# Delta rule's scan: the next batch's inverse ahead of the last merge, and the keys' turns next to the whole products

## The chip, the cores and the metric

One Trainium2 chip, one of its cores. The time is what one execution of the whole program takes on the device, in microseconds; the median of three runs is compared.

## What is computed

A trunk of two mixing layers over 1024 latent and 256 context tokens of width 1024, all in float32. The first layer has two branches, the second branch being a delta rule (RWKV-7) with 8 heads of 64, run once forward and once backward. Cut to what matters here:

```python
def rwkv_scan(inputs, S):
    def step(S, xs):
        r, v, kk, w, k, a = xs
        sa = jnp.einsum('bhvk,bhk->bhv', S, -kk)
        S = S * w[:, :, None, :] + sa[..., None] * (kk * a)[:, :, None, :] + v[..., None] * k[:, :, None, :]
        return S, jnp.einsum('bhvk,bhk->bhv', S, r)

    S, ys = lax.scan(step, S, tuple(jnp.moveaxis(t, 2, 0) for t in inputs))
    return jnp.moveaxis(ys, 0, 2), S
```

Each token rewrites a 64 x 64 state per head; the result is the state read by r. Everything else of the two layers (projections, the other scans, a long convolution, norms, output products) is in the program too and is not touched.

## The kernel before

The program is a row of stages, each with one block of code per engine; TensorE, VectorE, ScalarE and GpSimd take their instructions in the order in which that engine's block writes them, and wait on semaphores. `stage_rwkv_scan` runs twice, for d = 0 (forward) and d = 1 (backward). It takes the 1280 tokens in chunks of 64, two chunks (lanes 0 and 1) make a batch b, and there are 10 batches to a direction. 8 heads lie as 4 pairs j times 2 halves q of the partitions, so most products are groups of 8 or 16 matmuls of 64 x 64; in the trace a float32 matmul of this kind counts twice.

Inside a chunk the delta rule is a triangular system. Its inverse is built level by level for both lanes of a batch at once. Two buffers hold `inv` (upper and lower form), by b % 2. For batch b:

- `products(b, lane)` (TensorE, lines 1572 and 1578): keys times queries into the banks TURN and TURN + 1, and the strictly triangular products into STRICT. VectorE's `read_products` (line 1791) masks the first into `prod`.
- `begin_inverse(b, lane)` (VectorE, lines 1798, 1803 twice, 1806): copies the strict products out and sets level 0 of the inverse. It needs the products of its own batch and lane and `inv` filled by GpSimd.
- five levels n: `half_product(b, n)` (TensorE, line 1649), `copy_half` (ScalarE, line 1717), `whole_products(b, n)` (TensorE, line 1661, and for n < 5 line 1667), then `merge_upper` and `merge_lower` (VectorE, lines 1810 and 1814, predicated copies).
- `turns(b, lane)` (TensorE): four transposes of the keys into TURN (line 1590) and four of v into TURN + 1 (line 1594); ScalarE copies them out in `copy_keys` (line 1721) and `copy_v` (line 1726).

While batch b's inverse is built, the state is carried through batch b - 1, one lane in each half of the batch: `begin_chunk` (the states' products, line 1611), VectorE's `add_rest` (line 1822), `solve_chunk` (line 1620), ScalarE's `copy_u` (line 1738), `end_chunk` (lines 1629, 1634, 1638), VectorE's `update_state` (lines 1827, 1828). `pull(b)` (line 1602, copied by line 1733) prepares the next batch's right side. For d = 1 VectorE also adds the outputs (`add_y`, line 1835), for d = 0 ScalarE copies them (line 1744).

The order of the work is written out by hand in the loops over b at the end of each engine's block. The two waits that the change touches are these:

```python
pe.wait_ge(products_read, 4 * (b + 1) if lane == 0 else min(4 * (b + 1) + 2, 2 * N))   # ahead of the keys' turns
pe.wait_ge(level0_ready, 2 * (b + 1))                                                  # before half_product(b, 1)
```

`products_read` counts two for every `read_products`: lane 0's keys' turns wait for the reads of batch b, lane 1's for those of batch b + 1, lane 0, whose matmuls wrote the same bank. `level0_ready` counts one for every `begin_inverse`, so the first half product of a batch waits for both lanes' starts.

Of the kernel before, what the change touches and what calls it, by code (L numbers as in the profile page):

```python
# [19 lines left out]
P = 128  # L20
# [1452 lines left out]
def stage_rwkv_scan(p, arena, d, operands, v_dram, vT, chunk_decay, y):  # L1473
# [6 lines left out]
    nc = p.nc  # L1480
    C, J = R_CHUNK, R_PAIRS
# [3 lines left out]
    N = len(steps)  # L1485
    B = N // 2
# [7 lines left out]
    products_read = p.semaphore("r_products_read")  # L1494
# [8 lines left out]
    keys_turned = p.semaphore("r_keys_turned")  # L1503
# [18 lines left out]
    with ExitStack() as local:  # L1522
# [23 lines left out]
        with nc.Block() as block:  # L1546
# [13 lines left out]
            def _(pe):  # L1560
# [18 lines left out]
                                                keys(s)[part(q), j, q, :], start=True, stop=True)  # L1579
                    last.then_inc(strict_ready, 1)  # L1580

                def turns(b, lane):
                    s, c = 2 * b + lane, steps[2 * b + lane]

                    if d == 0 and s == 0:
                        pe.wait_ge(v_loaded, 32)
                        pe.wait_ge(pads_cleared, 2)
                    pe.wait_ge(products_read, 4 * (b + 1) if lane == 0 else min(4 * (b + 1) + 2, 2 * N))
                    for j in range(J):
                        last = nc.tensor.transpose(bank(TURN)[:, j * P:(j + 1) * P],  # L1590
                                                   keys(s)[:, j].rearrange("p k t -> p (k t)"), p.const("ident"))
                    last.then_inc(keys_turned, 1)
                    for j in range(J):
                        last = nc.tensor.transpose(bank(TURN + 1)[:, j * P:(j + 1) * P], vT[:, j, c * C:c * C + 2 * C], p.const("ident"))
                    last.then_inc(v_turned, 1)
# [77 lines left out]
                for b in range(B):  # L1673
                    half_product(b, 1)
                    if b:
                        begin_chunk(b - 1, 0)
                    whole_products(b, 1)
                    if b:
                        solve_chunk(b - 1, 0)
                    turns(b, 0)  # L1680
                    half_product(b, 2)
                    if b:
                        end_chunk(b - 1, 0)
                    whole_products(b, 2)
                    if b + 1 < B:
                        products(b + 1, 0)
                    half_product(b, 3)
                    if b:
                        begin_chunk(b - 1, 1)
                    whole_products(b, 3)  # L1690
                    if b:
                        solve_chunk(b - 1, 1)
                    turns(b, 1)
                    half_product(b, 4)
                    if b:
                        end_chunk(b - 1, 1)
                    whole_products(b, 4)
                    if b + 1 < B:
                        products(b + 1, 1)
                    half_product(b, 5)  # L1700
                    pull(b)
                    whole_products(b, 5)
# [73 lines left out]
            @block.vector  # L1776
            def _(dve):
                made = [0]

                def then(instruction):  # L1780
                    made[0] += 1
                    instruction.then_inc(chain, 1)
                    dve.wait_ge(chain, made[0])

                def read_products(b, lane):
                    s = 2 * b + lane
                    dve.wait_ge(products_ready, s + 1)
                    if b >= 2:
                        dve.wait_ge(outputs_ready, s - 3)
                    for q in range(2):  # L1790
                        nc.vector.tensor_tensor(prod[:, b % 2, lane, q], paired(bank(TURN + q)), product_mask(q), ALU.mult).then_inc(products_read, 1)

                def begin_inverse(b, lane):
                    s = 2 * b + lane
                    dve.wait_ge(strict_ready, s + 1)
                    if b >= 2:
                        dve.wait_ge(half_ready, TOP * (b - 1))
                    nc.vector.tensor_tensor(strict_t[:, b % 2, lane], narrow(bank(STRICT)[:, lane * HALF:(lane + 1) * HALF]),
                                            strict, ALU.mult).then_inc(strict_read, 1)
                    dve.wait_ge(inverse_filled, b + 1)  # L1800
                    dve.wait_ge(products_read, 2 * (s + 1))
                    for q in range(2):
                        nc.vector.copy_predicated(inv[part(q), b % 2, 0, lane], added(0, 0, J)[part(q)],
                                                  prod[part(q), b % 2, lane, q, :, part(q)])
                    dve.wait_ge(strict_read, s + 1)
                    nc.vector.copy_predicated(inv[:, b % 2, 1, lane], added(0, 1, J), strict_t[:, b % 2, lane]).then_inc(level0_ready, 1)  # L1806

                def merge_upper(b, n):
                    dve.wait_ge(upper_ready, TOP * b + n)
                    nc.vector.copy_predicated(flat(inv[:, b % 2, 0]), added(n, 0, 2 * J), narrow(bank(UPPER))).then_inc(upper_merged, 1)  # L1810

                def merge_lower(b, n):
                    dve.wait_ge(lower_ready, (TOP - 1) * b + n)
                    nc.vector.copy_predicated(flat(inv[:, b % 2, 1]), added(n, 1, 2 * J), narrow(bank(LOWER))).then_inc(lower_merged, 1)

                def add_rest(b, lane):
                    s = 2 * b + lane
                    dve.wait_ge(rest_ready, s + 1)
                    dve.wait_ge(pulled_copied, b + 1)
                    if s:  # L1820
                        dve.wait_ge(u_summed, s)
                    nc.vector.tensor_tensor(rest[:, :, :], pulled[:, lane], narrow(bank(CHAIN)[:, 0:HALF]), ALU.add).then_inc(rest_copied, 1)

                def update_state(b, lane):
                    s, c = 2 * b + lane, steps[2 * b + lane]
                    dve.wait_ge(update_ready, s + 1)
                    then(nc.vector.tensor_tensor(state[:, :, :], state[:, :, :], narrow(bank(CHAIN)[:, 0:HALF]), ALU.add))
                    nc.vector.tensor_tensor(
                        state[:, :, :], state[:, :, :], chunk_decay[:, :, c].unsqueeze(2).broadcast_to([P, J, C]), ALU.mult).then_inc(state_ready, 1)

                def add_y(b, lane):
                    if d == 1:
                        c = steps[2 * b + lane]
                        dve.wait_ge(outputs_ready, 2 * b + lane + 1)
                        nc.vector.tensor_tensor(y[:, c], y[:, c], narrow(bank(OUT)[:, 0:HALF]), ALU.add).then_inc(y_copied, 1)

                nc.vector.memset(state[:, :, :], 0.0).then_inc(state_ready, 1)
                dve.wait_ge(masks_loaded, 16)
                for lane in range(2):
                    read_products(0, lane)  # L1840
                    begin_inverse(0, lane)
                for b in range(B):
                    if b:
                        add_rest(b - 1, 0)
                    merge_upper(b, 1)
                    merge_lower(b, 1)
                    if b:
                        update_state(b - 1, 0)
                    merge_upper(b, 2)
                    merge_lower(b, 2)  # L1850
                    if b:
                        add_y(b - 1, 0)
                    if b + 1 < B:
                        read_products(b + 1, 0)
                    if b:
                        add_rest(b - 1, 1)
                    merge_upper(b, 3)
                    merge_lower(b, 3)
                    if b:
                        update_state(b - 1, 1)  # L1860
                    if b + 1 < B:
                        begin_inverse(b + 1, 0)
                    merge_upper(b, 4)
                    merge_lower(b, 4)
                    if b:
                        add_y(b - 1, 1)
                    if b + 1 < B:
                        read_products(b + 1, 1)
                    merge_upper(b, 5)
                    if b + 1 < B:  # L1870
                        begin_inverse(b + 1, 1)
                for lane in range(2):
                    add_rest(B - 1, lane)
                    update_state(B - 1, lane)
                    add_y(B - 1, lane)
# [1223 lines left out]
```

## Time and profile before

| | us |
|---|---|
| median of 3 runs | 3166.31 (3166.16 to 3173.97) |
| the profiled execution | 3175.72 |
| its span in the trace | 3173.9 |
| TensorE busy | 2769.6 (87% of the span) |
| VectorE busy | 1346.6 (42%) |
| ScalarE busy | 797.9 (25%) |
| GpSimd busy | 126.3 (4%) |

The profile is that of one execution. Its page gives for each engine the busy time, then groups of instructions by line with the time that the engine was idle just before them and what ended that idle time. The timeline gives single instructions in order; where many of one kind follow one another it merges them, with their number. PE is TensorE's matmuls, PEld its weight loads, DVE VectorE, ACT ScalarE, POOL GpSimd, and SPq the queue that issues transfers. The two directions of the scan lie between about 1010 and 1620 us of the span; the first full batches run from 1023 on (d = 0) and from 1327 on (d = 1).

### The profile page before, as it was taken

To read this page: it belongs to the slowest core of one execution; us is meant where nothing else is said; L and a number is where in the kernel's file an instruction comes from. 1 tells how busy PE (TensorE), PEld (TensorE's weight loads), DVE (VectorE), ACT (ScalarE), POOL (GpSimd) and SP (SyncE) were. 2 spreads that over 40 slices of the span, in tenths; PEclk is the share of its full clock that TensorE was granted. 3 is DMA by queue.
4 is the path that set the end of the run, shared out by engine and by line. 5 is a ranking of instruction groups with operands and counts; after the bars stand their busy time and mean duration, and the time that the engine had idled before them with its cause. 6 is when DMAs were issued, how large, how long until landed. Compare 5 with 4: busy or idle time off the path is not lost. (4 is left out here: it accounts for less than half of the span.)

```text
span 3173.9 us, 52024 instructions
## 1 busy us (share of the span) xinstructions
PE 2769.6 (87%) x23220; PEld 1767.4 (56%) x23220; DVE 1346.6 (42%) x2127; ACT 797.9 (25%) x1422; POOL 126.3 (4%) x133
## 2 busy tenths in 40 slices
PE   7899999998996898788847987996877999989678
PEld 2454566665453888788844423442433768677643
DVE  3220444433774554455560232224342566656614
ACT  2111222253563222222221021011100333343311
POOL 0000000000222000000001000002100000000000
PEclk9899999998997999899978997996988999999879
DMA  6200211112567110111014361101103000010033
GB/s 231 75 27 5 63 45 45 53 47 86 137 166 177 49 43 17 63 36 37 16 68 179 106 239 66 53 0 32 53 27 98 27 21 21 1 40 1 14 146 93
DMA packets 89788, 214.65 MB, mean 68 GB/s; under 512 B 6245, under 2 KB 45285, under 8 KB 85978
## 3 DMA queue, kind: packets, MB, share of 16 engines
q1 hardware_dynamic: 79854, 173.97, 15.9%
q0 software_dynamic: 9712, 37.36, 4.6%
q8 instruction: 183, 3.00, 0.4%
q14 instruction: 39, 0.32, 0.0%
HBM read 156.26 MB, written 55.05 MB: 67 GB/s over the span
## 5 line engine op out<-in xcount | busy, mean ns | idle before, releaser
L689 PE MATMUL psum<-arena,m_fill_weight 128*128 128x512 f32 (+1 forms) x864 | 335.5, 529 | 5.9 <-DMA m_fill_weight<-in_l_w_in 5.9
L2307 PE MATMUL psum<-arena,g_weight 128*128 128x512 f32 (+1 forms) x512 | 222.7, 562 | 26.1 <-DMA g_weight<-in_l_w_in 26.1
L389 PE MATMUL psum<-arena,project_weight_y 128*128 128x512 f32 x512 | 221.4, 595 | 13.0 <-DMA project_weight_y<-in_l_w_in 13.0
L689 PEld LDWEIGHTS psum<-arena,m_fill_weight 128*128 128x128 f32 x864 | 157.1, 193 | 108.2 <-issue 91.8
L389 PEld LDWEIGHTS psum<-arena,project_weight_y 128*128 128x128 f32 x512 | 97.8, 191 | 137.4 <-issue 122.8
L389 PE MATMUL psum<-arena,project_weight_m 128*128 128x512 f32 (+3 forms) x432 | 156.6, 525 | 14.9 <-DMA project_weight_m<-in_l_w_in 14.9
L2553 DVE COPY_PREDICATED g_pairs<-g_masks,psum 128x512 f32<-128x512 uint8 x128 | 93.5, 730 | 147.6 <-PE psum L2335 147.6
L1649 PE MATMUL psum<-r_inv,r_strict_t 64*64 64x64 f32 x3200 | 114.9, 222 | 46.8 <-DVE r_inv L1806 46.8
L1166 PE MATMUL psum<-gp_weight,arena 128*128 128x512 f32 x320 | 149.9, 617 | 0.0
L2298 PE MATMUL psum<-g_weight,arena 128*128 128x128 f32 x1152 | 145.0, 275 | 0.0
L2057 PE MATMUL psum<-out_weight,arena 128*128 128x512 f32 x256 | 115.0, 613 | 28.1 <-DMA out_weight<-in_l_w_out 28.1
L2066 PE MATMUL psum<-out_weight,arena 128*128 128x512 f32 x320 | 137.7, 592 | 0.0
L1717 ACT COPY r_half<-psum 128x512 f32<-128x512 f32 x100 | 58.5, 585 | 313.8 <-PE psum L1649 313.8
L2298 PEld LDWEIGHTS psum<-g_weight,arena 128*128 128x128 f32 x1152 | 136.7, 192 | 0.0
L1649 PEld LDWEIGHTS psum<-r_inv,r_strict_t 64*64 64x64 f32 x3200 | 102.9, 136 | 56.5 <-DVE r_inv L1806 49.7
L2307 PEld LDWEIGHTS psum<-arena,g_weight 128*128 128x128 f32 x512 | 92.2, 200 | 74.1 <-issue 49.8
L389 PEld LDWEIGHTS psum<-arena,project_weight_m 128*128 128x128 f32 (+1 forms) x432 | 82.0, 190 | 90.1 <-issue 69.1
L1661 PE MATMUL psum<-r_half,r_inv 64*64 64x64 f32 x3200 | 121.4, 229 | 12.2 <-ACT r_half L1717 12.0
L2335 PEld LDWEIGHTS psum<-arena 128*128 128x128 f32 x896 | 120.3, 205 | 16.9 <-issue 15.7
L2335 PE MATMUL psum<-arena 128*128 128x128 f32 x896 | 127.2, 289 | 0.0
L2099 DVE TENSOR_TENSOR out_res<-psum,out_gate 128x1024 f32<-128x1024 f32 x18 | 22.0, 1224 | 233.7 <-PE psum L2057 147.5
L1810 DVE COPY_PREDICATED r_inv<-r_masks,psum 128x512 f32<-128x512 uint32 x100 | 72.8, 728 | 113.5 <-PE psum L1661 113.5
(382 smaller groups left out, 4338.2 us busy)
## 6 DMA issues: line engine op xcount, KB each, us to landing
mod_weight<-in_l_mod_w SPq DMA_DIRECT2D x16, 1536.0 KB, 7.7
arena<-scratch_operands SPq DMA_DIRECT2D x40, 512.0 KB, 3.6
scratch_operands<-arena POOLq DMA_DIRECT2D x16, 640.0 KB, 8.2
scratch_operands<-arena POOLq DMA_DIRECT2D x32, 320.0 KB, 11.2
g_weight<-in_l_w_in SPq DMA_DIRECT2D x20, 512.0 KB, 4.3
m_fill_weight<-in_l_w_in SPq DMA_DIRECT2D x18, 512.0 KB, 3.8
out_weight<-in_l_w_out SPq DMA_DIRECT2D x16, 512.0 KB, 11.4
project_weight_y<-in_l_w_in SPq DMA_DIRECT2D x4, 2048.0 KB, 7.9
```

Of the source, the lines that this page charges most:

```text
L389: last = nc.tensor.matmul(p.psum[0:rows, u % 8, 0:n], lhsT, rhs, start=(k == 0), stop=(k == KT - 1))
L689: last = nc.tensor.matmul(p.psum[:, FILL + f % BANKS, 0:width], weight[:, q % PIECES, k, :], hT[:, k, at:at + width], start=(k == 0), stop ...
L1166: last = nc.tensor.matmul(p.psum[:, PROJECT + u % 2, :], hT[:, k, t * P:(t + 1) * P], weight[:, job, k, :], start=(k == 0), stop=(k == KT ...
L1649: last = nc.tensor.matmul(bank(H_BANK)[part(q), at(lane, j)], strict_t[part(q), b % 2, lane, j, :], inv[part(q), b % 2, 0, lane, j, :], st ...
L1661: last = nc.tensor.matmul(bank(UPPER)[part(q), at(lane, j)], inv[part(q), b % 2, 1, lane, j, :], half[part(q), lane, j, :], start=True, st ...
L1810: nc.vector.copy_predicated(flat(inv[:, b % 2, 0]), added(n, 0, 2 * J), narrow(bank(UPPER))).then_inc(upper_merged, 1)
L2057: last = nc.tensor.matmul(p.psum[:, 2 * i + n, :], lhsT, weight[:, k, n * BANK:(n + 1) * BANK], start=(k == 0), stop=(k == KT - 1))
L2066: last = nc.tensor.matmul(p.psum[:, 2 * (i % 4) + n, :], lhsT, weight[:, k, n * BANK:(n + 1) * BANK], start=(k == 0), stop=(k == KT - 1))
L2298: last = nc.tensor.matmul(bank[:, (t - part[0]) * P:(t - part[0] + 1) * P], hT[:, kk, t * P:(t + 1) * P], w[:, kk, :], start=(kk == 0), st ...
L2307: last = nc.tensor.matmul(bank[:, 0:width], w[:, kk, :], hT[:, kk, first:first + width], start=(kk == 0), stop=(kk == KT - 1))
L2335: last = nc.tensor.matmul(p.psum[:, SCORES + m % RING, (c - 4 * g) * C:(c - 4 * g + 1) * C], left, right, start=True, stop=True)
L2553: nc.vector.copy_predicated(pairs[:, w % 2, 4 * g:4 * g + 4, :], mask(units[w][1], n), chunked(p.psum[:, SCORES + m % RING, :])).then_inc( ...
```

## The change

Two edits, both of order. No instruction is new and none is gone.

- `turns` is cut in two: `turn_keys` (with its wait for `products_read`) and `turn_v` (with the waits for v's load and the cleared pads, for the first chunk of d = 0). In each half of a batch `turn_keys` now stands ahead of `whole_products(b, 1)` and `whole_products(b, 3)`, and `turn_v` stays behind `solve_chunk`, where both stood.
- On VectorE `begin_inverse(b + 1, 1)` stands ahead of `merge_upper(b, 5)`, no longer behind it.

```diff
-                def turns(b, lane):
-                    s, c = 2 * b + lane, steps[2 * b + lane]
-
-                    if d == 0 and s == 0:
-                        pe.wait_ge(v_loaded, 32)
-                        pe.wait_ge(pads_cleared, 2)
+                def turn_keys(b, lane):
+                    s = 2 * b + lane
                     pe.wait_ge(products_read, 4 * (b + 1) if lane == 0 else min(4 * (b + 1) + 2, 2 * N))
                     for j in range(J):
                         last = nc.tensor.transpose(bank(TURN)[:, j * P:(j + 1) * P],
                                                    keys(s)[:, j].rearrange("p k t -> p (k t)"), p.const("ident"))
                     last.then_inc(keys_turned, 1)
+
+                def turn_v(b, lane):
+                    s, c = 2 * b + lane, steps[2 * b + lane]
+
+                    if d == 0 and s == 0:
+                        pe.wait_ge(v_loaded, 32)
+                        pe.wait_ge(pads_cleared, 2)
                     for j in range(J):
@@ TensorE's loop, lane 0; the same for lane 1 around whole_products(b, 3)
                     if b:
                         begin_chunk(b - 1, 0)
+                    turn_keys(b, 0)
                     whole_products(b, 1)
                     if b:
                         solve_chunk(b - 1, 0)
-                    turns(b, 0)
+                    turn_v(b, 0)
                     half_product(b, 2)
@@ VectorE's loop
                     if b + 1 < B:
                         read_products(b + 1, 1)
+                        begin_inverse(b + 1, 1)
                     merge_upper(b, 5)
-                    if b + 1 < B:
-                        begin_inverse(b + 1, 1)
```

VectorE's queue at the end of a batch, before (r_prod is the masked product, r_strict_t the strict products, r_inv the inverse, r_rest the right side for the solve):

```order
L1791 TENSOR_TENSOR r_prod<-psum,r_masks 128x512 x2
L1810 COPY_PREDICATED r_inv<-r_masks,psum 128x512
L1798 TENSOR_TENSOR r_strict_t<-psum,r_masks 128x256
L1803 COPY_PREDICATED r_inv<-r_masks,r_prod 64x256 x2
L1806 COPY_PREDICATED r_inv<-r_masks,r_strict_t 128x256
L1822 TENSOR_TENSOR r_rest<-r_pulled,psum 128x256
```

The same place in the changed kernel, whose VectorE lines lie 5 further down (1791 is 1796):

```order
L1796 TENSOR_TENSOR r_prod<-psum,r_masks 128x512 x2
L1803 TENSOR_TENSOR r_strict_t<-psum,r_masks 128x256
L1808 COPY_PREDICATED r_inv<-r_masks,r_prod 64x256 x2
L1811 COPY_PREDICATED r_inv<-r_masks,r_strict_t 128x256
L1815 COPY_PREDICATED r_inv<-r_masks,psum 128x512
L1827 TENSOR_TENSOR r_rest<-r_pulled,psum 128x256
```

The merge of level 5 (1810, now 1815) went from ahead of begin_inverse's four instructions to behind them.

TensorE's queue from the first half product of a batch to the second, before (consts is the identity of a transpose, arena holds the keys, r_vT v):

```order
L1649 MATMUL psum<-r_inv,r_strict_t 64x64 x16
L1611 MATMUL psum<-r_state,arena 64x64 x8
L1661 MATMUL psum<-r_half,r_inv 64x64 x16
L1667 MATMUL psum<-r_inv,r_half 64x64 x16
L1620 MATMUL psum<-r_rest,r_inv 64x64 x8
L1590 MATMUL psum<-consts,arena 128x128 x4
L1594 MATMUL psum<-consts,r_vT 128x128 x4
L1649 MATMUL psum<-r_inv,r_strict_t 64x64 x16
```

The same place in the changed kernel (1649 is 1652 now, 1590 is 1586):

```order
L1652 MATMUL psum<-r_inv,r_strict_t 64x64 x16
L1614 MATMUL psum<-r_state,arena 64x64 x8
L1586 MATMUL psum<-consts,arena 128x128 x4
L1664 MATMUL psum<-r_half,r_inv 64x64 x16
L1670 MATMUL psum<-r_inv,r_half 64x64 x16
L1623 MATMUL psum<-r_rest,r_inv 64x64 x8
L1597 MATMUL psum<-consts,r_vT 128x128 x4
L1652 MATMUL psum<-r_inv,r_strict_t 64x64 x16
```

The four transposes of the keys went from behind the solve to between the states' products and the whole products; those of v stayed. ScalarE's, GpSimd's and the transfers' queues have the same order in both kernels.

## Rows read from the trace of the kernel before

**Rows 1.** The page's costliest groups: line, tiles, shape, count | busy, mean ns | idle before.
```profile
L1649 PE MATMUL psum<-r_inv,r_strict_t 64*64 64x64 f32 x3200 | 114.9, 222 | 46.8 <-DVE r_inv L1806 46.8
...
L1661 PE MATMUL psum<-r_half,r_inv 64*64 64x64 f32 x3200 | 121.4, 229 | 12.2 <-ACT r_half L1717 12.0
```

**Rows 2.** Timeline, TensorE: start, length, operation, count [idle before <- releaser].
```profile
1051.96 1.15 PE L1649 MATMUL psum<-r_inv,r_strict_t 64*64 64x64 f32 x32 [2.39 <-DVE r_inv L1806]
...
1080.05 1.15 PE L1649 MATMUL psum<-r_inv,r_strict_t 64*64 64x64 f32 x32 [2.39 <-DVE r_inv L1806]
...
1081.88 1.97 PE L1661 MATMUL psum<-r_half,r_inv 64*64 64x64 f32 x32
...
1109.36 1.15 PE L1649 MATMUL psum<-r_inv,r_strict_t 64*64 64x64 f32 x32 [2.39 <-DVE r_inv L1806]
...
1583.91 1.15 PE L1649 MATMUL psum<-r_inv,r_strict_t 64*64 64x64 f32 x32 [2.39 <-DVE r_inv L1806]
```

**Rows 3.** Windows, two batches: PE, PEld, DVE, ACT, POOL busy; PEclk; DMA share; GB/s.
```profile
1052.00:1080.00 28.00, 25.22 (x720) 23.63 (x720) 14.45 (x27) 8.37 (x18) 1.05 (x1) 1.00 0.13 41
1080.00:1109.30 29.30, 26.70 (x720) 25.13 (x720) 14.44 (x27) 8.37 (x18) 1.05 (x1) 0.94 0.12 39
```

**Rows 4.** Timeline, all engines, a batch's end in the second direction.
```profile
1407.65 1.27 DVE L1791 TENSOR_TENSOR r_prod<-psum,r_masks 128x512 f32<-128x512 f32 x2
...
1409.48 1.15 PE L1661 MATMUL psum<-r_half,r_inv 64*64 64x64 f32 x32
...
1409.60 0.58 ACT L1733 COPY r_pulled<-psum 128x512 f32<-128x512 f32 x1 [0.18 <-PE psum L1602]
...
1410.67 0.72 DVE L1810 COPY_PREDICATED r_inv<-r_masks,psum 128x512 f32<-128x512 uint32 x1 [1.75 <-PE psum L1661]
...
1411.29 0.41 DVE L1798 TENSOR_TENSOR r_strict_t<-psum,r_masks 128x256 f32<-128x256 f32 x1
...
1412.51 0.45 DVE L1806 COPY_PREDICATED r_inv<-r_masks,r_strict_t 128x256 f32<-128x256 uint32 x1
...
1413.01 1.15 PE L1649 MATMUL psum<-r_inv,r_strict_t 64*64 64x64 f32 x32 [2.39 <-DVE r_inv L1806]
```

**Rows 5.** Timeline, VectorE, the last merge of a batch, first direction.
```profile
1077.71 0.72 DVE L1810 COPY_PREDICATED r_inv<-r_masks,psum 128x512 f32<-128x512 uint32 x1 [2.08 <-PE psum L1661]
```

**Rows 6.** Timeline, all engines, the second lane's piece of that batch.
```profile
1394.73 1.16 PE L1572 MATMUL psum<-arena 64*128 64x128 f32 x16
...
1395.94 1.29 DVE L1791 TENSOR_TENSOR r_prod<-psum,r_masks 128x512 f32<-128x512 f32 x2
...
1397.27 0.63 PE L1611 MATMUL psum<-r_state,arena 64*64 64x64 f32 x16
...
1397.48 0.58 ACT L1717 COPY r_half<-psum 128x512 f32<-128x512 f32 x1 [4.67 <-PE psum L1649]
...
1398.12 1.15 PE L1661 MATMUL psum<-r_half,r_inv 64*64 64x64 f32 x32 [0.22 <-ACT r_half L1717]
...
1399.10 1.10 PE L1667 MATMUL psum<-r_inv,r_half 64*64 64x64 f32 x32
...
1400.04 0.63 PE L1620 MATMUL psum<-r_rest,r_inv 64*64 64x64 f32 x16
...
1400.60 0.66 PE L1590 MATMUL psum<-consts,arena 128*128 128x128 f32 x4
...
1401.09 0.60 PE L1594 MATMUL psum<-consts,r_vT 128*128 128x128 f32 x4
...
1401.49 0.58 ACT L1721 COPY r_k_tok<-psum 128x512 f32<-128x512 f32 x1
...
1401.62 0.97 PE L1649 MATMUL psum<-r_inv,r_strict_t 64*64 64x64 f32 x26
...
1402.82 0.59 ACT L1717 COPY r_half<-psum 128x512 f32<-128x512 f32 x1 [0.74 <-PE psum L1649]
```

**Rows 7.** Timeline, TensorE, first batch of the second direction.
```profile
1341.65 1.15 PE L1661 MATMUL psum<-r_half,r_inv 64*64 64x64 f32 x32 [0.69 <-ACT r_half L1717]
```

More of the change, by code:

```diff
@@ L1689, in _ @@
                         begin_chunk(b - 1, 1)
+                    turn_keys(b, 1)
                     whole_products(b, 3)
@@ L1692, in _ @@
                         solve_chunk(b - 1, 1)
-                    turns(b, 1)
+                    turn_v(b, 1)
                     half_product(b, 4)
```

## The prediction

> **What bounds the kernel now.** I read the page first, for the share of the engines. TensorE is busy for 87% of the span (table above), so anything that shortens TensorE's queue, or a stall of it, counts in full unless another engine is close behind. I then went to the groups of instructions [rows 1]. Two groups of the scan's matmuls have idle time of TensorE before them: 46.8 us before the half products of line 1649, released by VectorE's line 1806 (the last step of begin_inverse), and 12.2 us before the whole products of line 1661, released by ScalarE's copy of line 1717. Those two are what the edit aims at.
>
> The timeline of TensorE's queue says where the first one stands [rows 2]. From the second batch of a direction on, the first half product of each batch waits 2.39 us; there are 9 such waits in each direction, 18 in all, 43.0 us (the others are the two starts, 1.92 us each, that the change leaves). The starts of these rows also give the batch period: 28.09 us (1051.96 to 1080.05) for 12 batches and 29.2 to 29.4 for 6 (the first of them is 1080.05 to 1109.36, 29.31); of the 18 waits the row at 1051.96 is the first and that at 1583.91 the last. The six long ones differ in one thing [rows 3]: the granted clock is 0.94 over the batch, where it is 1.00 in its neighbour. In it the whole products that began at 1081.88, just after the wait of 2.39 us, took 1.97 us [rows 2] for what takes 1.15 in other batches [rows 6]: TensorE was at 1.2 GHz for a stretch, then at 2.4 again. I find such a fall in the six batches only, behind the same stall each time.
>
> The timeline of a batch's end shows why VectorE is late [rows 4]. It finishes the products' reads (line 1791, 1407.65 + 1.27 = 1408.92), then waits 1.75 us for the last whole products, merges them (line 1810), and only then takes begin_inverse, lines 1798 to 1806, from 1411.29 to 1412.96. TensorE starts the next batch at 1413.01. Nothing that begin_inverse reads comes from the last merge: its inputs were there when VectorE went idle. In the first direction, without add_y on VectorE, the idle stretch is longer, 2.08 us [rows 5].
>
> **The change part by part.** No instruction is added or removed on any engine; two pieces are moved, and no DMA is.
>
> *begin_inverse ahead of the last merge.* It takes 1412.96 - 1411.29 = 1.67 us [rows 4]. Put behind the reads it begins at about 1408.84 (on VectorE a follower starts some 0.08 us before the end of the row ahead, as line 1798 does behind 1810) and ends at 1410.51. The last whole products begin at 1409.48; a run of 32 such matmuls hands over after 0.98 us (1398.12 to 1399.10 [rows 6]), so TensorE is free at 1410.46. VectorE's signal, 0.05 us behind its end as now, comes at 1410.56. The half product then starts at 1410.56 where it started at 1413.01: 2.45 us in the second direction. In the first VectorE has 0.33 us more room, TensorE sets the start, and it gains 1413.01 - 1410.46 = 2.55. Sum: 9 x 2.45 + 9 x 2.55 = 45.0 us. The merge itself is pushed back by nothing: the whole products end at 1410.63 and VectorE is free at 1410.51, a cover of 0.12 us; were that cover gone, its result is first wanted by the next whole products (for the PSUM bank), about 2 us later (half products 0.98, states' products 0.56, keys' turns 0.49, as worked out below), while the merge takes 0.72. Behind the moved wait for the strict products stands only that merge; line 1578 has ended before the reads are over, so the wait is met.
>
> *The clock.* With the stall gone TensorE has at most 0.1 us of idle time there, and the six falls lose what preceded them. Each costs 29.31 - 28.09 = 1.22 us [rows 2]: 6 x 1.2 = 7.2 us. Bounds: 0 if the falls come anyway, 7.2 if none does. I take 7.2, since all six stand behind that stall and none elsewhere in a full batch.
>
> *The keys' turns.* One piece of a batch now [rows 6]: the states' products begin at 1397.27, whole products at 1398.12 (0.85 later; 0.22 of that waits for ScalarE's copy, 1397.48 + 0.58 = 1398.06), the second whole products 1399.10, the solve 1400.04, keys' turns 1400.60, v's turns 1401.09, the next half product 1401.62: 4.35 us. With the keys' turns moved: states' products 0.56 (a group of 16 as the solve: 1400.04 to 1400.60), keys' turns 0.49, whole 0.98 and 0.94, solve 0.56, v's turns 0.53: 4.06 us. The gain is 0.29 us, since 0.49 us of turns fill a hole of 0.29 and push the whole products back by 0.20. It happens twice in each of 18 batches: 36 x 0.29 = 10.4 us. Bounds: 0, if the later whole products are felt at once somewhere, and 36 x 0.49 = 17.6, if the turns were hidden whole. I take 10.4, which the starts give.
>
> Who might feel it? ScalarE: its copy of the keys (line 1721, behind that of u) ends at 1401.49 + 0.58 = 1402.07, and the next copy of a half product starts at 1402.82, after 0.74 us of idle time [rows 6]. The half product comes 0.49 us nearer to the solve, so 0.25 us of that room is left. The keys' turns now wait earlier for VectorE's reads of the other lane's products: these run from 1395.94 for 1.29 us, to 1397.23, and the turn is due at 1397.27 + 0.56 = 1397.83, 0.60 us of room. In the other lane the reads end at 1408.92 and the turn is due near 1412.1.
>
> *The first batch of a direction.* There is no states' product, and whole products wait 0.69 us [rows 7]; the turns fit into that hole. 4 turns x 0.49 = 2.0 us.
>
> **The sum**: 45.0 + 7.2 + 10.4 + 2.0 = 64.6 us. The profiled execution took 3175.7 us, which gives 3111.1. The median of the runs is 3166.31, 9.4 us less, and I take the difference as the same for both kernels: 3101.7. One of three runs of before was at 3173.97, so a median some 8 us higher is possible and belongs in the range.
>
> **A rule against it.** The keys' turns ran at the full clock: 4 of them took 0.66 us behind the solve and the half product behind them kept its pace [rows 6]. The Trainium skill (TensorE: Matmul & The Clock Gate, Part 4: PE-mode transpose) says that a transpose does not count as work for the clock gate as other matmuls do; the trace does not agree so far, and it is a rival below.
>
> **The rivals.**
> 1. *The keys' turns give nothing*, the rest works. ScalarE's 0.25 us of room is little. For it: four ScalarE operations follow one another there. Against: the room comes out positive with 0.25 us, and line 1717's copy takes 0.58 to 0.59 us each time [rows 6]. Time: 3101.7 + 12.4 = 3114. Chance 0.12.
> 2. *The stall is passed on.* TensorE starts earlier and meets another wait in the next piece, most likely the one for the pulled products or the rest. These are copied at 1409.60 + 0.58 = 1410.18 [rows 4], and wanted at 1410.56 + 0.98 = 1411.54, so 1.4 us of room speaks against it. If half of the 45 us came back, the time would be 3124, and with the falls of the clock too, 3131. Chance 0.07.
> 3. *The turns cost the clock.* If each keys' turn, now cut off from v's, brought one fall, 36 x 1.22 = 44 us would come back: 3146. Forty pairs of turns without a fall behind them speak against. Chance 0.03. It is the case that the page's rule would give.
> 4. *Slower: the keys' turn blocks TensorE's queue.* Its wait for VectorE's reads stands ahead of the whole products now, so a late read holds up all of the chain and with it the merges. Place: lane 1, room 0.60 us. To cancel 64.6 us over 18 batches it needs 3.6 us of stall each, so reads that end 4.2 us later than now; at 5 us later the time is 3101.7 + 18 x 4.4 = 3181. But the reads start 0.05 us behind the products' matmuls (1394.73 + 1.16 = 1395.89 [rows 6]), which stand on TensorE's own queue ahead of the turn, so a reader can hardly fall behind; I give it 0.01.
> 5. *The wait is not lifted*, since another semaphore holds the half product or begin_inverse. The order of both queues shows the move, the buffer of the fill by GpSimd and the strict products are done earlier; then only 12.4 us would be won, 3154. Chance 0.02.
>
> **How the numbers follow.** The forecast has 0.75; its own range is 3094 to 3110: 5 us for the keys' term, 7 for the clock, 8 for the spread of the runs. With rival 1 the range is 3093 to 3117, and what is left out is rivals 2 to 5, 0.13, and the tails. About 0.3% (9.5 us) is what a measurement of this kernel can tell from no change. Forecast and rivals 1, 2, 3 and 5 are all faster by more; rival 4 is slower; to no change I give 0.02 for gains eaten by something I don't see. Faster 0.97, same 0.02, slower 0.01.
>
> **What would show it.** In the profile after: no idle time of TensorE before the half products except at the two starts and at most 0.1 us in the second direction; VectorE idle ahead of the last merge near 0.1 us in the second direction and 0.4 in the first; no wait of the whole products on ScalarE's copy from the second batch on; batches of 25.0 us (28.09 - 2.5 - 0.6) in place of 28.09, all with a granted clock of 1.00. I am wrong if batches are longer than 25.5 us, if falls of the clock stay, or if a wait appears before the keys' turns.

## The result, and the profile after

The changed kernel took 3115.85 us (median of 4 runs, 3110.89 to 3121.62) beside 3170.14 us for the kernel before (4 runs, 3166.16 to 3175.87): ratio 0.9828, 95% interval 0.9801 to 0.9855. Three later comparisons of the same two kernels gave 3111.70 to 3173.23, 3114.34 to 3177.51 and 3109.91 to 3174.00, ratios 0.9804, 0.9806 and 0.9796. So the change is worth 54 to 64 us, against a forecast of 64.6. Direction and mechanism were right. The time of 3101.7 us was 8 to 14 us too low: 3115.85 lies outside the range of the forecast itself (3094 to 3110) and inside the wider one (3093 to 3117) that also takes in rival 1; the later medians, 3109.91 to 3114.34, lie on both sides of 3110.

The page of the changed kernel, costliest groups (line, tiles, shape, count | busy, mean ns | idle before), answers to [rows 1]; line 1649 is now 1652, line 1661 is 1664:

```profile
L1664 PE MATMUL psum<-r_half,r_inv 64*64 64x64 f32 x3200 | 115.6, 222 | 2.9 <-ACT r_half L1722 2.7
L1652 PE MATMUL psum<-r_inv,r_strict_t 64*64 64x64 f32 x3200 | 114.2, 222 | 3.8 <-DVE r_inv L1811 3.8
```

The idle time before the half products fell from 46.8 us to 3.8, which is the two starts (1.92 each) and nothing else; that before the whole products fell from 12.2 to 2.9, of which four waits of 0.69 us in the first batches are 2.7. The whole products' mean duration is lower too, 222 ns for 229 (the half products had 222 already): no stretch at half clock is left in the full batches. The windows over one batch of each direction show it (PE, PEld, DVE, ACT, POOL busy; PEclk; DMA share; GB/s), where [rows 3] had 25.2 to 26.7 us of work in 28.0 to 29.3:

```profile
1075.20:1100.40 25.20, 25.20 (x728) 23.55 (x724) 14.49 (x27) 8.37 (x18) 1.04 (x1) 1.00 0.13 45
...
1371.60:1397.00 25.40, 25.40 (x724) 23.66 (x722) 15.12 (x29) 7.62 (x16) 1.04 (x1) 1.00 0.14 45
```

TensorE is busy for all of it. The end of a batch, timeline of all engines, first direction (rows 1074.30 to 1075.49) and second (1370.48 to 1371.67), answers to [rows 4, 5]:

```profile
1074.30 1.15 PE L1664 MATMUL psum<-r_half,r_inv 64*64 64x64 f32 x32
...
1074.56 0.45 DVE L1811 COPY_PREDICATED r_inv<-r_masks,r_strict_t 128x256 f32<-128x256 uint32 x1
1075.28 1.10 PE L1652 MATMUL psum<-r_inv,r_strict_t 64*64 64x64 f32 x32
1075.49 0.73 DVE L1815 COPY_PREDICATED r_inv<-r_masks,psum 128x512 f32<-128x512 uint32 x1 [0.48 <-PE psum L1664]
...
1370.48 1.15 PE L1664 MATMUL psum<-r_half,r_inv 64*64 64x64 f32 x32
...
1371.07 0.45 DVE L1811 COPY_PREDICATED r_inv<-r_masks,r_strict_t 128x256 f32<-128x256 uint32 x1
1371.57 1.15 PE L1652 MATMUL psum<-r_inv,r_strict_t 64*64 64x64 f32 x32
1371.67 0.73 DVE L1815 COPY_PREDICATED r_inv<-r_masks,psum 128x512 f32<-128x512 uint32 x1 [0.15 <-PE psum L1664]
```

The last whole products hand over to the next batch's half products after 0.98 us in the first direction and 1.09 in the second, where VectorE's line 1811 ends at 1371.52, 0.05 us before the start. The merge is not later: it starts 1.19 us behind the start of the last whole products in both directions, as before (1409.48 to 1410.67), and VectorE has 0.48 and 0.15 us of idle time ahead of it.

The other piece, TensorE's timeline from one half product to the next, answers to [rows 6]:

```profile
1062.22 0.63 PE L1614 MATMUL psum<-r_state,arena 64*64 64x64 f32 x16
1062.79 0.66 PE L1586 MATMUL psum<-consts,arena 128*128 128x128 f32 x4
1063.37 1.15 PE L1664 MATMUL psum<-r_half,r_inv 64*64 64x64 f32 x32
1064.36 1.10 PE L1670 MATMUL psum<-r_inv,r_half 64*64 64x64 f32 x32
1065.29 0.63 PE L1623 MATMUL psum<-r_rest,r_inv 64*64 64x64 f32 x16
1065.85 0.65 PE L1597 MATMUL psum<-consts,r_vT 128*128 128x128 f32 x4
1066.44 0.97 PE L1652 MATMUL psum<-r_inv,r_strict_t 64*64 64x64 f32 x26
```

From the states' products to the next half product it is 4.22 us, where it was 4.35 and where the prediction had 4.06. The keys' turns, alone now, hand over after 0.58 us and v's after 0.59, not after 0.49 and 0.53 as they did side by side.

One more reading is needed before the experiments. I take the scan from the first to the last of ScalarE's 20 copies of the pulled products (line 1733, now 1738), one per batch. It lasted 556.9 us before (1048.55 to 1605.41) and 495.9 after (1049.21 to 1545.10): 61.0 us less. The profiled executions differ by 54.1 us (3175.72 and 3121.62), so about 7 us were lost outside that stretch. The stretch leaves out the first batch of the first direction, up to its copy, and takes in what lies between the two directions: 57.8 of the 61.0 us are in the nine intervals between copies of each direction, 3.2 between the two directions.

### The profile page after: what moved, and what is told of

It is laid out like the page before. It is cut to its first block and busy times, and to the rows that moved or that the text cites. A ratio compares the mean times of both kernels' runs of the same rounds, so it can differ in the third digit from the quotient of the medians.

```text
span 3119.8 us, 52024 instructions
## 1 busy us (share of the span) xinstructions
PE 2769.6 (89%) x23220; PEld 1760.4 (56%) x23220; DVE 1347.2 (43%) x2127; ACT 798.4 (26%) x1422; POOL 126.4 (4%) x133
## 5 line engine op out<-in xcount | busy, mean ns | idle before, releaser
L215 PE MATMUL psum<-mod_weight,mod_silu 128*2 128x512 f32 x192 | 90.2, 622 | 28.3 <-DMA mod_weight<-in_l_mod_w 28.3
```

The costliest lines, as they stand in the source:

```text
L215: last = nc.tensor.matmul(p.psum[0:2, g, :], silu[:, i, :], weight[:, i % SLOTS, g * BANK:(g + 1) * BANK], start=(i == 0), stop=(i == KT - 1))
```

## The experiments

The batch periods below are the intervals between those copies in each profile; a direction has 8 of them before its last, shorter one.

| kernel | median, us | before, measured beside it | ratio (95%) | periods, first direction | second direction | scan |
|---|---|---|---|---|---|---|
| before | | | | 28.09, three of 29.3 | 28.09, three of 29.2 to 29.5 | 556.9 |
| changed, again | 3111.70 | 3173.23 | 0.9804 (0.9789 to 0.9819) | 25.21 | 25.38 | 495.9 |
| inverse only | 3117.99 | 3173.23 | 0.9824 (0.9809 to 0.9839) | 25.48 | 25.65 | 502.6 |
| keys only | 3168.39 | 3173.23 | 0.9980 (0.9966 to 0.9994) | 27.81, five of 29.0 to 29.3 | 27.80, two of 29.3 | 553.6 |
| stall filled, 18 | 3200.23 | 3173.23 | 1.0082 (1.0067 to 1.0098) | 29.84 | 29.84 | 581.2 |
| stall filled, 10 | 3167.28 | 3174.00 | 0.9976 (0.9966 to 0.9986) | 28.10 | 28.10 | 547.4 |
| changed, third | 3114.34 | 3177.51 | 0.9806 (0.9786 to 0.9825) | 25.21 | 25.37 | 495.1 |
| pair in the hole | 3108.03 | 3177.51 | 0.9778 (0.9757 to 0.9798) | 24.62 | 24.79 | 484.7 |
| keys early | 3138.26 | 3177.51 | 0.9880 (0.9863 to 0.9897) | 26.49 | 26.66 | 519.3 |
| pair, sum late | 3107.08 | 3177.51 | 0.9782 (0.9764 to 0.9800) | 24.62 | 24.49 to 24.78 | 484.0 |
| changed, fourth | 3109.91 | 3174.00 | 0.9796 (0.9779 to 0.9813) | 25.21 | 25.38 | 496.1 |
| pair, again | 3110.34 | 3174.00 | 0.9793 (0.9775 to 0.9812) | 24.62 | 24.79 | 484.2 |

**The changed kernel again.** No edit.

> The changed kernel once more, on the same chip as the next three. Theory: the scan's batches repeat to 0.01 us (25.21 us in the first direction, 25.38 in the second, clock 1.00), so the scan is 61 us shorter than before again, and what the first profile lost outside the scan (7.0 us, of 54.1 us in all) is the spread of the other stages from execution to execution: it will be a different number here, between -5 and +8 us. Rival: the loss outside the scan belongs to the change (a shifted start of the later stages) and comes back as 6 to 8 us.

The scan was 495.9 us once more, with the same periods to 0.01 us. Span less scan was 2623.9 us in the first profile of this kernel (3119.8 - 495.9), and 2614.2, 2616.8 and 2611.3 in the three later ones: one kernel spreads over 12.6 us outside the scan. For the kernel before it was 2617.0, so the second profile of the change is 2.8 us below it. The 7 us lost in the first comparison belong to that spread; the rival, that the change itself causes them, is out.

**The inverse alone.** The diff to the kernel before:

```diff
                     if b + 1 < B:
                         read_products(b + 1, 1)
+                        begin_inverse(b + 1, 1)
                     merge_upper(b, 5)
-                    if b + 1 < B:
-                        begin_inverse(b + 1, 1)
```

> Before, with begin_inverse ahead of the last merge and the turns left together. Theory: the 18 waits of 2.39 us go (45 us) and the six falls of the clock with them (7 us): about 52 us under before, batches of 28.09 - 2.56 = 25.53 us in the first direction and 25.65 in the second, the waits of 0.22 us on ScalarE's copy still there. Rival: the two moves need each other, and a good part of the stall stays without the keys' turns: batches over 26 us.

55.2 us under before, with batches of 25.48 and 25.65 us. This one move is nearly all of the result. The waits on ScalarE's copy stayed, as the page's group of the whole products shows:

```profile
L1661 PE MATMUL psum<-r_half,r_inv 64*64 64x64 f32 x3200 | 116.5, 223 | 13.4 <-ACT r_half L1717 13.4
```

Their idle time is 13.4 us here, 12.2 before: it is longer because six of the waits had been swallowed by the falls of the clock. The rival, that the two moves need each other, is out.

**The keys' turns alone.** The changed kernel, with begin_inverse put back behind the last merge:

```diff
-                        begin_inverse(b + 1, 1)
                     merge_upper(b, 5)
+                    if b + 1 < B:
+                        begin_inverse(b + 1, 1)
```

> Before, with the keys' turns moved and begin_inverse left behind the last merge. Theory: the waits of 2.39 us stay, and falls of the clock behind them (four to eight in all); each half of a batch gains 0.13 to 0.20 us, not the predicted 0.29: batches of 27.76 us, 5 to 8 us under before with the first batches. Rival: the turns give the predicted 0.29 us twice when they are alone (batches of 27.51, 12 us under before), or nothing.

4.8 us under before; the batches without a fall of the clock are 27.81 us, 0.28 shorter. That is 0.14 us for each half of a batch, half of the predicted 0.29. The profile's list of waits has the 2.39 us untouched (us in total, times, longest):

```profile
PE psum L1652 <- DVE r_inv L1811: 46.8, 20, 2.4
```

Two of the 20 are the starts. With the stall still there the falls stay too: seven long periods among the 16, and the last one of the first direction also (26.14 where the second direction has 24.62), eight in all for the six of before. So the falls go with the stall, and not with the old place of the turns. Why 6 of 18 equal stalls bring a fall in one trace and 8 of 18 in the other, the runs do not show.

**The stall filled.** The kernel before, with matmuls whose result nobody uses in TensorE's queue at the place of the stall. Every output is computed as before.

```diff
                     if n == 1:
+                        if b:
+                            for i in range(18):
+                                nc.tensor.matmul(bank(H_BANK)[:, 0:P], p.const("ident"), p.const("ident"), start=True, stop=True)
                         pe.wait_ge(level0_ready, 2 * (b + 1))
```

> Before, with 18 matmuls of the identity (128 x 128, result not used) in TensorE's queue ahead of each batch's first half product, where it waits 2.39 us; the wait itself stays, since begin_inverse still ends when it does. Theory: the falls of the clock come from TensorE being without work there, so they vanish although the batch is no shorter than 28.09 us: all batches at 28.1 and clock 1.00, about 7 us under before. Rival: the falls have to do with the rhythm of the batches or of other work, and the six of 29.2 to 29.4 us stay, with a time as before.

This was a miss: 27.0 us slower where 7 us faster were expected. The trace counts 36 matmuls per batch at this line and they take 4.29 us, which is longer than the hole and makes every batch 29.84 us long, 1.75 us more than before:

```profile
1079.39 4.29 PE L1646 MATMUL psum<-consts 128*128 128x128 f32 x36
```

Of the falls it says the same already: no batch is longer than another by more than 0.01 us, and the clock is 1.00. The second attempt has `range(10)`.

> The filled stall with 10 matmuls in place of 18. The first filling took 4.2 us where the hole is 2.5 (each of these float32 matmuls shows as two of 0.12 us), so it made every batch 29.84 us. Ten take 2.4 us and fit. Theory: all batches at 28.1 us and clock 1.00, no falls, the scan 7 us shorter than before's. Rival: falls of the clock come back in some batches, as in the kernel before.

Timeline of all engines, end of a batch in the first direction:

```profile
1070.93 1.15 PE L1664 MATMUL psum<-r_half,r_inv 64*64 64x64 f32 x32
...
1072.01 2.50 PE L1646 MATMUL psum<-consts 128*128 128x128 f32 x20
...
1073.98 0.45 DVE L1809 COPY_PREDICATED r_inv<-r_masks,r_strict_t 128x256 f32<-128x256 uint32 x1
...
1074.49 1.15 PE L1652 MATMUL psum<-r_inv,r_strict_t 64*64 64x64 f32 x32
```

The half products still begin 0.06 us behind VectorE's line 1809, as in the kernel before, and 3.56 us behind the last whole products, where [rows 4] have 3.53. But TensorE has work in between. Windows over eight batches, the kernel before first, the filled one below it:

```profile
1048.50:1276.80 228.30, 206.35 (x5764) 193.90 (x5766) 115.62 (x216) 66.97 (x145) 8.37 (x8) 0.98 0.10 31
```

```profile
1043.00:1267.80 224.80, 221.31 (x5924) 207.83 (x5924) 115.75 (x216) 67.03 (x145) 8.37 (x8) 1.00 0.10 32
```

The clock is 1.00 over all of it, every period is 28.10 us, and the eight batches take 224.8 us for 228.3. Over the 18 periods of both directions this is 7.1 us, and the median is 6.7 us under before (interval of the ratio 0.9966 to 0.9986). The scan of this profile is 9.5 us shorter (547.4 for 556.9); the other 2.4 us lie between the directions, where no filling was added, and can't come from it. With 36 stalls filled in two traces and no fall, against 6 and 8 falls in 18 open stalls each, TensorE at 1.2 GHz was a consequence of its having nothing to do in the stall; work that is of no use is enough to keep it at 2.4 GHz. The Trainium skill (TensorE: Matmul & The Clock Gate, Part 1: The HAM clock gate) says that the default state is the throttled one and activity releases it; the fill runs agree (clock 1.00 over the eight batches with the filling, 0.98 without).

**The keys' turn one step earlier**, a dose of the rival that a wait blocks TensorE's queue. The diff to the changed kernel:

```diff
+                    turn_keys(b, 1)
                     half_product(b, 3)
                     if b:
                         begin_chunk(b - 1, 1)
-                    turn_keys(b, 1)
                     whole_products(b, 3)
```

> The changed kernel with lane 1's keys' turns one step earlier, ahead of the third half product. A dose of the rival that the keys' turn blocks TensorE's queue: VectorE's reads of the same bank end 0.94 us after the place. Theory: TensorE waits 0.94 us there in each batch, and the hole of 0.29 us ahead of the whole products opens again: 1.2 us per batch, 22 us over 18 batches; batches of 26.4 us. Rival: the wait is absorbed, since the levels of the inverse have slack elsewhere: under 5 us.

23.9 us slower than the changed kernel measured beside it, batches 1.28 us longer: about the theory's 22 and 1.2. The waits between 1060 and 1280 us name the place:

```profile
PE psum L1586 <- DVE r_prod L1796: 6.2, 8, 0.8
...
PEld psum L1664 <- ACT r_half L1722: 3.2, 9, 0.4
```

TensorE waits 0.8 us in each batch for VectorE's reads (0.94 was expected), nothing absorbs it, and the hole ahead of the whole products is open again. The mechanism of the slower rival is real, one step away from where the change put the turns; at the change's own place no such wait appears, so the room of 0.60 us holds.

**Both turns ahead of the whole products.** The diff to the changed kernel, the same in the other half of a batch:

```diff
                     turn_keys(b, 0)
+                    turn_v(b, 0)
                     whole_products(b, 1)
                     if b:
                         solve_chunk(b - 1, 0)
-                    turn_v(b, 0)
@@ turn_v
+                    if s:
+                        pe.wait_ge(v_copied, s)
```

The added wait keeps v's turns off a bank that ScalarE is still copying from, in the last batch.

> The changed kernel with v's turns moved too, right behind the keys' turns and ahead of the whole products. Theory: what the prediction missed is that a group of turns hands over to another group of turns after 0.49 us but to 64-row matmuls only after 0.58; with the turns adjacent again that is paid once per piece and not twice, so each piece takes 4.14 us where it takes 4.22: batches of 25.05 us, 3 us under the changed kernel. Rival: ScalarE has no room for a half product that comes a further 0.59 us nearer to the solve (its copy of the half product starts 0.3 us late), and the whole products of levels 2 and 4 wait: batches as now or longer.

Batches of 24.62 and 24.79 us, 0.59 us under the changed kernel where I expected 0.16 (25.05 us). TensorE's timeline of the piece:

```profile
1088.37 0.63 PE L1616 MATMUL psum<-r_state,arena 64*64 64x64 f32 x16
1088.93 0.66 PE L1586 MATMUL psum<-consts,arena 128*128 128x128 f32 x4
1089.43 0.60 PE L1599 MATMUL psum<-consts,r_vT 128*128 128x128 f32 x4
1089.96 1.15 PE L1666 MATMUL psum<-r_half,r_inv 64*64 64x64 f32 x32
1090.94 1.10 PE L1672 MATMUL psum<-r_inv,r_half 64*64 64x64 f32 x32
1091.87 0.63 PE L1625 MATMUL psum<-r_rest,r_inv 64*64 64x64 f32 x16
1092.34 0.93 PE L1654 MATMUL psum<-r_inv,r_strict_t 64*64 64x64 f32 x26
```

3.97 us, where the changed kernel has 4.22 and before 4.35; the rest of the 0.59 us lies behind it, from the half product to the next whole products, which takes 2.41 us (1092.34 to 1094.75) for 2.46 in each half of a batch. The turns side by side hand over after 0.50 and 0.53 again. What I had not counted is the other side: the solve hands over to a half product of its own shape after 0.47 us, and to turns after 0.56. So a switch between groups of 64 x 64 and of 128 x 128 costs some 0.05 to 0.1 us each way, and the change has four switches where the pair has two. It is not special to transposes: in the filled stall the plain matmuls of 128 x 128 begin 1.07 us behind the whole products (1078.32 to 1079.39), where a 64 x 64 group begins after 0.98. What in the switch costs the time (the shape, or the weights that go with it) no run separates. ScalarE had enough room, though little: its copy of the half product starts 1.47 us behind the half product, 0.28 later than in the changed kernel, as the rival had it, but ends at 1094.40 and the whole products begin at 1094.75.

The scan is 10.4 us shorter than the changed kernel's (484.7 for 495.1), but the medians of whole executions differ by 6.3 us, and by nothing in the repeat, next to a fourth profile of the changed kernel:

> The changed kernel beside the next, on the same chip: 52 to 66 us under before.

> Both turns ahead of the whole products once more. Its scan was 10.4 us shorter than the changed kernel's, but the median of whole executions only 6.3. Theory: the rest is the spread of the stages outside the scan, so the two medians of this call differ by 10 us with some 5 either way. Rival: something outside the scan gives it back, and the difference stays at 6 or under.

3110.34 against 3109.91, although the scan was 11.9 us shorter in the profiles (484.2 for 496.1), whose spans differ by 5.9 us (3101.5 for 3107.4). The expected 10 us, some 5 either way, were missed, and the rival, that something outside the stretch gives the time back, has the measured difference. Outside the scan the profiles of this variant took 2625.7 and 2617.3 us, and the next variant 2625.2, within what the changed kernel shows or just above it (2611.3 to 2623.9).

A part of it has a cause that the traces show. In the first batch of the first direction v's turns wait for the transfer that brings v, and the stretch that I call the scan begins only behind that batch. With the pair these turns stand earlier, so the wait is longer and the whole products are now behind it. The changed kernel of the first comparison, then the pair:

```profile
1031.43 0.66 PE L1597 MATMUL psum<-consts,r_vT 128*128 128x128 f32 x4 [0.52 <-DMA r_vT<-scratch_spill]
```

```profile
1029.35 1.11 PE L1599 MATMUL psum<-consts,r_vT 128*128 128x128 f32 x4 [4.45 <-DMA r_vT<-scratch_spill]
```

In the three profiles with the pair the wait is 4.26 to 4.65 us, and the batch takes 28.05 to 29.21 us from its first half product to its copy; in the four of the changed kernel the wait is at most 2.29 us and the batch takes 24.16 to 26.59. The means differ by 3.4 us. Another part is noise that lies ahead of all this: that first half product starts anywhere from 1015 to 1024 us in these seven profiles. Behind the last copy the pair took 1572.1 to 1574.6 us and the changed kernel 1568.5 to 1574.7; whether that difference is more than chance, these runs don't tell. What is shown is a shorter scan with a dearer first batch, not a faster program.

**The second lane's sum later**, on top of the pair:

```diff
                     merge_lower(b, 4)
-                    if b:
-                        add_y(b - 1, 1)
                     if b + 1 < B:
                         read_products(b + 1, 1)
                         begin_inverse(b + 1, 1)
                     merge_upper(b, 5)
+                    if b:
+                        add_y(b - 1, 1)
```

> The kernel with both turns ahead of the whole products, and on VectorE the second lane's sum of outputs (0.40 us, second direction alone) behind the last merge. Theory: in the second direction VectorE no longer sets the start of the next batch, so its batches come down to the first direction's (0.15 us each, 1.4 us in all), 4 to 5 us under the changed kernel in sum. Rival: the sum behind the merge holds up the right side of the next solve and gives the time back.

> The changed kernel on the chip of the next three, as their yardstick: batches of 25.21 and 25.38 us, 52 to 62 us under before.

Five of the eight periods of the second direction are 24.62 us here, the first direction's, for 24.79 without the move, so VectorE mostly no longer sets the start. The gain of about 1 us is far below what the medians can show (3107.08 for 3108.03).

## Why the prediction was right, and where it was off

- **The stall, 45.0 us: right.** TensorE gained 3.54 - 0.98 = 2.56 us per batch in the first direction (1076.51 to 1080.05 in the trace of before, 0.98 after) and 3.53 - 1.09 = 2.44 in the second, 9 of each: 45.0 us. The inverse alone shows it by itself. The start by VectorE in the second direction was foreseen to 0.01 us.
- **The clock, 7.2 us: right.** No period in the changed kernel is long, in four profiles, and the filled stall alone gave back 7.1 us of the scan.
- **The keys' turns, 10.4 us: the mechanism right, the size double.** The step that failed is the piece's sum with "keys' turns 0.49" and "v's turns 0.53: 4.06 us", from which 0.29 us per piece follow. I took the pace of turns that stand next to turns for turns that stand alone. Alone they cost 0.58 and 0.59, the piece is 4.22, and inverse alone against both moves gives 25.48 - 25.21 = 0.27 us per batch: 18 x 0.27 = 4.9 us.
- **The first batches, 2.0 us:** four of the eight waits of 0.69 us are gone, as forecast. The size can't be read off as cleanly, since the second direction's first batch begins at 1.2 GHz (half products 1.97 us where they take 1.15) and the return to 2.4 comes at another point in each execution. From first half product to copy the second direction's took 25.26 us before and 25.22 with the inverse alone, and 22.75 to 23.46 in the four profiles of the change, which is 1.8 to 2.5 us for 1.0; but it took 23.87 with the stall filled by 10, where this batch is as before. The first direction's also waits for v.
- **The period, forecast 25.0 us:** 25.21 and 25.38, the keys' term and the second direction's 0.12.
- **The base.** Profile against profile the forecast was 3111.1 us for an execution that took 3121.62. Of these 10.5 us the scan explains 3.6 (61.0 for 64.6, of which 1.0 was forecast for the first direction's first batch, ahead of that stretch), and what lies outside 6.9. The 3.6 are small by luck: the keys' term alone was 5.5 too high, and about 2 us came back in the second direction's first batch and ahead of it. The median of three that I carried the sum over to, 3166.31, was also on the low side: 3170.14 with one more run, 3173 to 3178 in later comparisons. Against those the gain was 61.5, 63.2 and 64.1 us.
- **The rivals.** That the keys' turns give nothing is refuted (0.27 us per batch, repeated), although the first median, 3115.85, lies near rival 1's 3114: it is there by the spread outside the scan. ScalarE kept 0.31 us of idle time ahead of the copy in question, where 0.25 was forecast. The stall was not passed on: TensorE is busy for 25.20 of 25.20 us. Turns alone cost no fall of the clock: 1.00 in every full batch of the changed kernel, so the statement of the Trainium skill (TensorE: Matmul & The Clock Gate, Part 4: PE-mode transpose) that the prediction names has no consequence here. The blocked queue did not occur, and was made to occur by one step more. That the wait isn't lifted is refuted too: no wait of 2.39 us is left.
- **Two slips in reading**, without effect on the sum: between the starts of these rows there are 10 periods of 28.09 us and 6 long ones, not 12 and 6, and line 1798 starts 0.10 us before the end of 1810's row (1411.39), not 0.08.

## What to carry to other kernels

A stall of a few microseconds that repeats in every turn of a loop can be worth more than its own length when TensorE is the one that waits (here 45 us and 7 more for the clock): look at the granted clock of neighbouring turns, and test with work of no use in the hole. Before an instruction is moved into a hole, read its length among neighbours like those it will have: the same four turns took 0.49 us beside turns and 0.58 between matmuls of another shape. When one queue is full for all of a period, only work taken off it counts, or an order with fewer switches between kinds of matmul. Differences of 10 us in one stage need the stage's own rows, since the rest of this program spreads by as much; and the rows must take in the loop's first turn, where a moved instruction can meet a transfer that the others never wait for.

## What the runs showed that was not expected

- Useless matmuls made the kernel faster, by 6.7 us, without moving a wait.
- A change between 64 x 64 and 128 x 128 in TensorE's queue has a price: solve to half product 0.47 us, solve to turns 0.56; turns to turns 0.49 to 0.50, turns to 64 x 64 matmuls 0.53 to 0.59.
- The better order in the loop's full batches cost 3.4 us in its first one, where v had not yet landed.
- What lies outside the scan took 2611.3 to 2623.9 us in four profiled executions of one kernel, while the scan repeated to 1 us (495.1 to 496.1).
